# A sparse-attention decoder step: sampled queries broadcast by DMA, their logits eight units earlier

## The chip, the cores and the metric

The kernel is written for one Trainium2 chip and runs on one of its cores. Its time is the time of the whole program on the device in microseconds; the median of several runs counts. A core has TensorE (PE, matmuls and transposes into PSUM), VectorE (DVE), ScalarE (ACT), GpSimd (POOL) and SyncE (SP); the last two issue most of the DMAs here. Each engine works through its own list in order and waits on semaphores.

## The reference

One layer of a hybrid decoder, for 1024 prompt tokens and 8 sampled tokens (one each of 8 sequences with 2048 cached positions). Only the attention matters here. For each query an indexer has chosen 256 keys; the query attends over these alone:

```
q, k, v = project(x)                          # 8 heads of 64, rotary on a quarter of each head
idx = top_k(index_scores, 256)
ks, vs = rows idx of the keys and values      # samples: from the paged cache, or the sample's own new row
logits = einsum('bthd,btkhd->bthk', q, ks) * 64 ** -0.5
out = einsum('bthk,btkhd->bthd', softmax(logits), vs)
```

Everything is float32. Behind it come the merge of the branches, a layer norm, a router and a mixture of 32 experts.

## The kernel before

The program is a row of blocks with a barrier of all engines between two of them. `project_and_score` computes q, k, v and the index scores, `choose_keys_and_gate` picks the keys and computes the gates, `attend` is the attention, and `merge_route_and_experts` begins with loads of the gates (L1553) and matmuls with the weights `w_a` (L1643).

**Prompt.** `attend` goes over 32 units `(t, hp)`: tiles of 128 queries t = 7, 6, ... 0, and in each the four pairs of heads. Unit n of t has logits of 128 queries by (t+1)*128 keys for two heads. So units 0 to 3 have t = 7, units 8 to 11 t = 5, units 12 to 15 t = 4, units 16 to 19 t = 3, units 28 to 31 t = 0. All engines go over the same steps s = 0 to 33, as a pipeline written out by hand. In step s:

- TensorE: `make_logits(s)` (L1173), which waits until VectorE has read the logits of unit s-1; transposes of the probabilities of unit s-1 (`turn_probs`, L1187; for t of 4 and more, the keys from 512 on come at the end of the step); `weigh(s-2)` with the values (L1200), which waits at each new t until the output bank has been read; at the last pair of a t, `spread_shares` (L1213).
- VectorE: masks, scales and takes the bound of the logits of unit s (L1385, one operation for each of two heads, and a short read of the accumulator); at times a reciprocal (L1390); copies a share of unit s-1's transposed probabilities out of PSUM (L1296); `share_out` (L1372) at the last pair of a t.
- ScalarE: the other copies (L1296), the exponentials (L1312), a copy of the shares (L1323).

Logits lie in PSUM banks 0 and 2, and, from 512 keys (t of 4 and more) on, in banks 1 and 3 too.

**Samples.** Their work is set between the steps. GpSimd gathers the 256 chosen rows of K and of V of each sample b from the cache by indirect DMA, in two halves of 128 rows (L1132), and one own row from the new keys and values (L1137); it issues a few of them in each unit, when `wait_for_turn` says that the unit's probabilities have been copied: K in units 0 to 7, own K and the first halves of V in units 8 to 15, the second halves and own V in units 16 to 23. K of the first four samples lies where `w_a` is loaded later. With `narrow` = 16 the steps are: in steps 18 to 25, one sample each, TensorE spreads the query over 128 partitions by a matmul of a broadcast column with the identity, into bank 1 or 3 (`spread_query`, L1222), and VectorE multiplies it with K and sums over each head (`sample_logits`, L1345 and L1347, twice each). In step 26 the logits are transposed (L1230) and their maximum is taken, in 27 ScalarE exponentiates, in 28 VectorE scales, in 29 the probabilities are transposed (L1236), in 30 TensorE weighs V with them (L1247). Behind the loop ScalarE copies the result (L1326), TensorE transposes it (L1258), and VectorE picks it into `attnT` in sixteen small copies (L1411). TensorE ends with the first matmuls with `w_a` (L1285), which wait for the last `share_out`. SP loads `w_a` once the first four samples' logits are done.

Of the kernel before, what the change touches and what calls it, by code (L numbers as in the profile page):

```python
# [16 lines left out]
ALU = mybir.AluOpType  # L17
# [50 lines left out]

def project_and_score(nc, ins, outs, keep):

# [4 lines left out]
    with nc.cleanup_on_exit(), ExitStack() as ctx:  # L75
# [91 lines left out]
        def _(sp):  # L167
# [16 lines left out]
            for t in range(2, NT):  # L184
# [7 lines left out]
                         zs[2 * FEW:2 * FEW + N_SAMPLE, IDX_HEADS * HD:(IDX_HEADS + 1) * HD]).then_inc(few_out, 16)  # L192
            sp.dma_start(outs["v_all"][SEQ:, :], zs[3 * FEW:3 * FEW + N_SAMPLE, :]).then_inc(few_out, 16)
            for t in range(NT):
                j = t % 2
                if t == NT - 1:
                    sp.wait_ge(acc_full, 1 + 4 * NT)
                    for k in range(KC // 2, KC):
                        sp.dma_start(keep["w_uv"](k), ins["w_uv"][:, k, :]).then_inc(keep["w_uv_in"][k], 16)
                sp.wait_ge(roped, t + 2)  # L200
                sp.dma_start(outs["k_all"][t * P:(t + 1) * P, :], z[j][:, AW:2 * AW]).then_inc(stored[j], 16)
                sp.dma_start(outs["kidx_all"][t * P:(t + 1) * P, :], z[j][:, (ROPE_HEADS - 1) * HD:ROPE_HEADS * HD]).then_inc(stored[j], 16)
                sp.wait_ge(acc_read, AFTER_FEW + 5 * t + 5)
# [11 lines left out]
            sp.wait_ge(few_out, 48)  # L215
            sp.wait_ge(rest_in, 16)
# [171 lines left out]
        def _(act):  # L388
# [11 lines left out]
            def read(t, g):  # L400
                bank = FIRST_BANKS[g] if t == 0 else g % 2
                act.wait_ge(acc_full, 1 + 4 * t + g + 1)
                if g == 0 and t == 1:
                    act.wait_ge(few_out, 48)
                    act.wait_ge(turned_full, 1)
# [628 lines left out]
def attend(nc, ins, outs, keep, scratch):  # L1034


    SCALE = HD ** -0.5
    PAIRS = HEADS // 2
    n_qh = N_SAMPLE * HEADS
    with nc.cleanup_on_exit(), ExitStack() as ctx:  # L1040
# [3 lines left out]
        def sem(name):  # L1044
            return nc.alloc_semaphore(name)
# [14 lines left out]
        own_b = sb("own_b", [1, N_SAMPLE], I32)  # L1060
        own_row = sb("own_row", [2, N_SAMPLE], U32)
        lg = sb("lg", [P, 2, n_qh])
        prob_s = sb("prob_s", [n_qh, TOPK])
# [18 lines left out]
        dve_step = sem("a_dve_step")  # L1082
        q_spread = sem("q_spread")
        lg_ready = sem("lg_ready")
# [8 lines left out]
        narrow = order.index(3) * PAIRS  # L1093
        query_at = {narrow + 2 + b: b for b in range(N_SAMPLE)}
        MAX_AT, EXP_AT, PROBS_AT, TURN_AT, WEIGH_AT = (max(query_at) + n for n in (1, 2, 3, 4, 5))

# [23 lines left out]
        @block.sync  # L1120
        def _(sp):
            wait_for_gates_stored(sp)
            sp.dma_start(first[:], ins["first_masks"]).then_inc(const_in, 16)
            sp.dma_start(own_b[:], ins["rank"][:, 0:N_SAMPLE]).then_inc(own_in, 16)
            sp.wait_ge(lg_ready, N_SAMPLE // 2)
            sp.dma_start(keep["w_a"][:], ins["w_a"]).then_inc(w_a_in, 16)
            sp.wait_ge(w_a_in, 16)

        @block.gpsimd
        def _(pool):  # L1130
# [13 lines left out]

            for b in range(N_SAMPLE):
                wait_for_turn(b)
                for half in range(2):
                    gather(k_of, "cache_k", b, half, k_in)
            pool.wait_ge(own_ready, 1)
            pool.wait_ge(k_in, 32 * N_SAMPLE)  # L1150
            for b in range(N_SAMPLE):
                wait_for_turn(N_SAMPLE + b)
                gather_own(k_of, "k_all", b, k_in)
                gather(v_of, "cache_v", b, 0, v_in)
            pool.wait_ge(v_in, 16 * N_SAMPLE)
            for b in range(N_SAMPLE):
                wait_for_turn(2 * N_SAMPLE + b)
                gather(v_of, "cache_v", b, 1, v_in)
                gather_own(v_of, "v_all", b, v_in)
            pool.wait_ge(k_in, 48 * N_SAMPLE)  # L1160
# [3 lines left out]
        def _(pe):  # L1164
# [52 lines left out]

            def spread_query(b):
                if b >= 2:
                    pe.wait_ge(lg_ready, b - 1)  # L1220
                for k in range(AW // P):
                    mm = nc.tensor.matmul(ps[:, 1 + 2 * (b % 2), k * P:(k + 1) * P],  # L1222
                                          qT[:, k, SEQ + b:SEQ + b + 1].to_broadcast([P, P]), ident[:],
                                          start=True, stop=True)
                mm.then_inc(q_spread, 1)

            def turn_sample_logits():
# [24 lines left out]
            def turn_sample_out():  # L1252
                wait_copied(pe, len(chunks) - 2)
                wait_copied(pe, len(chunks) - 1)
                for g in range(2):
                    pe.wait_ge(s_copied, g + 1)
                    for k in range(AW // P):
                        mm = nc.tensor.transpose(ps[:, TURN + g, k * P:(k + 1) * P], product[g][:, k * P:(k + 1) * P], ident[:])  # L1258
                    mm.then_inc(s_turned, 1)

            for s in range(LAST):
                if s < N:
                    make_logits(s)
                if s in query_at:
                    spread_query(query_at[s])
                if s == MAX_AT:
# [3 lines left out]
                if s == WEIGH_AT:  # L1270
                    weigh_sample()
                if 0 <= s - 1 < N:
                    turn_probs(s - 1, 0)
# [4 lines left out]
                if 0 <= s - 1 < N and units[s - 1][0] >= 4:  # L1278
                    turn_probs(s - 1, 4)
            turn_sample_out()  # L1280
            pe.wait_ge(w_a_in, 16)
# [18 lines left out]
        def _(act):  # L1300
            for s in range(LAST):
# [22 lines left out]
            for g in range(2):  # L1324
                act.wait_ge(s_out, g + 1)
                nc.scalar.copy(product[g][:], ps[:, 1 + 2 * g, :]).then_inc(s_copied, 1)  # L1326

        @block.vector
        def _(dve):
# [39 lines left out]
            def share_out(t):  # L1369
# [4 lines left out]
                                        shares[:].rearrange("p (k q) -> p k q", q=P), ALU.mult).then_inc(out_read, 1)  # L1374

            for s in range(LAST):
                if s < N:
# [27 lines left out]
            for g in range(2):  # L1405
                dve.wait_ge(s_turned, g + 1)
                for k in range(AW // P):
                    for odd in range(2):
                        q0 = odd * HD
                        mine = ps[q0:q0 + HD, TURN + g, k * P:(k + 1) * P].rearrange("p (j h) -> p j h", h=32)  # L1410
                        nc.vector.tensor_copy(attnT[q0:q0 + HD, k, SEQ + 4 * g:SEQ + 4 * (g + 1)], mine[:, :, 2 * k + odd])  # L1411

# [1058 lines left out]
def build(nc, ins, outs, scratch):  # L2471
    with ExitStack() as whole:
# [4 lines left out]
        with ExitStack() as mixer:  # L2477
# [9 lines left out]
            with nc.sbuf_tensor("x_all", [P, KC, SEQ + N_SAMPLE], F32, side="right") as keep["x_all"], \  # L2487
# [10 lines left out]
                keep["made_out"] = [whole.enter_context(nc.semaphore(f"made_out{j}")) for j in range(2)]  # L2498
                project_and_score(nc, ins, outs, keep)
                choose_keys_and_gate(nc, ins, outs, keep, scratch)  # L2500
# [121 lines left out]
```

## Time and profile before

| what | value |
| --- | --- |
| runs of the program | 1389.69, 1389.03, 1385.95 us, median 1389.03 |
| the profiled execution | 1389.41 us |
| its span, first to last instruction | 1388.0 us |
| mean granted TensorE clock | 0.986 of full |
| attention stage | from 678 to 829.5 us |
| TensorE, VectorE busy over the span | 1321.8, 720.9 us |

The page of the profile gives busy times, the chain of work that ended last, and the costliest groups of instructions. L1173 is a line of the kernel. The timeline gives, for one instruction or a merged row of equal ones, the start, the duration, the engine, the line, what is written from what, and in brackets how long the engine stood idle before it and what released it.

### The profile page before, as it was taken

How to read it: one execution, taken by the hardware profiler on the slowest of the kernel's cores; microseconds unless marked ns; L12 is line 12 of the kernel's file. 1: busy time of each engine (PE TensorE's matmuls, PEld its weight loads, DVE VectorE, ACT ScalarE, POOL GpSimd, SP SyncE). 2: the span in 40 equal slices, each digit the busy share in tenths (PEclk: the TensorE clock that was granted, in tenths of full speed). 3: DMA queues.
4: the chain of work that ended last, by engine and by line, in shares of the span. 5: the costliest groups of instructions: out<-in, count | busy, mean ns of one | idle time of the engine just before them, and what ended most of it. 6: DMA issues, size and time to landing. Idle time of an engine off the chain costs nothing. (4 is left out here: it accounts for less than half of the span.)

```text
span 1388.0 us, 19213 instructions
## 1 busy us (share of the span) xinstructions
PE 1321.8 (95%) x6689; PEld 680.6 (49%) x6689; DVE 720.9 (52%) x1709; ACT 280.3 (20%) x621; POOL 245.0 (18%) x292
## 2 busy tenths in 40 slices
PE   8999999899999999999899989999978999999984
PEld 2444444445466666666577656544443333333321
DVE  0211123589898888998265863588881111111135
ACT  0100112322221111111356430000001111111124
POOL 2222000043420000021134400011112111111113
PEclk9999999999999999999999999999989999999997
DMA  9311002210031111110132319931137999999936
GB/s 326 98 52 62 17 17 77 94 50 1 0 109 69 69 68 69 68 68 32 34 100 62 125 34 318 388 127 31 38 114 256 365 408 406 406 412 411 394 143 255
DMA packets 70316, 214.13 MB, mean 154 GB/s; under 512 B 16059, under 2 KB 41915, under 8 KB 59866
## 3 DMA queue, kind: packets, MB, share of 16 engines
q1 hardware_dynamic: 56266, 184.74, 35.5%
q0 software_dynamic: 12688, 27.76, 5.8%
q8 instruction: 52, 0.85, 0.2%
q10 hardware_dynamic: 1280, 0.53, 0.2%
q14 instruction: 30, 0.25, 0.1%
HBM read 186.47 MB, written 34.65 MB: 159 GB/s over the span
## 5 line engine op out<-in xcount | busy, mean ns | idle before, releaser
L262 PE MATMUL ps_mixer<-front,x_all 128*128 128x512 f32 (+1 forms) x448 | 180.4, 557 | 1.7 <-ACT wi L413 1.7
L959 DVE TENSOR_SCALAR_CACHE_REDUCE front<-score,bound 128x384 bf16<-128x384 f32 (+2 forms) x198 | 173.9, 940 | 0.4 <-DVE bound L981 0.3
L262 PEld LDWEIGHTS ps_mixer<-front,x_all 128*128 128x128 f32 x448 | 83.2, 190 | 91.7 <-issue 78.7
L2102 PE MATMUL ps<-w_gate_up,w_o 128*32 128x512 f32 (+1 forms) x640 | 114.9, 597 | 1.7 <-DVE w_o L2186 1.7
L1672 PE MATMUL ps<-w_o,mergedT 128*128 128x512 f32 x256 | 116.5, 601 | 0.0
L2102 PE MATMUL ps<-w_a,w_o 128*64 128x512 f32 (+1 forms) x256 | 114.8, 602 | 0.0
L787 PE MATMUL ps_mixer<-x_all,front 128*128 128x344 f32 x384 | 114.4, 453 | 0.0
L787 PE MATMUL ps_mixer<-x_all,w_gate 128*128 128x344 f32 x384 | 113.3, 453 | 0.0
L2211 DVE TENSOR_TENSOR w_o<-w_o,ps 128x256 f32<-128x256 f32 x24 | 10.1, 421 | 165.7 <-ACT w_o L2166 165.7
L787 PEld LDWEIGHTS ps_mixer<-x_all,w_gate 128*128 128x128 f32 x384 | 72.7, 190 | 37.5
L787 PEld LDWEIGHTS ps_mixer<-x_all,front 128*128 128x128 f32 x384 | 72.6, 190 | 37.1
L959 DVE TENSOR_SCALAR_CACHE_REDUCE front<-score_s,bound 8x2049 bf16<-8x2049 f32 x33 | 77.0, 2334 | 0.0
L941 POOL TENSOR_TENSOR front<-front 128x344 f32<-128x344 f32 x24 | 28.6, 1193 | 241.6 <-ACT front L901 241.6
L1672 PEld LDWEIGHTS ps<-w_o,mergedT 128*128 128x128 f32 x256 | 46.0, 190 | 47.8 <-issue 47.8
L2102 PEld LDWEIGHTS ps<-w_gate_up,w_o 128*32 128x32 f32 (+1 forms) x640 | 33.5, 116 | 70.2 <-issue 70.2
L2080 POOL DMA_INDIRECT pair_out<-w_o,entries x24 | 25.1, 1044 | 233.4 <-DVE w_o L2218 233.4
L898 ACT ACTIVATE front<-ps_mixer,gate_bias 128x344 f32<-128x344 f32 x48 | 26.2, 547 | 177.0 <-PE ps_mixer L787 177.0
L1643 PE MATMUL ps<-attnT,w_a 128*128 128x344 f32 x186 | 56.0, 464 | 3.4 <-DVE mergedT L1792 1.9
L2134 PE MATMUL ps<-gates,w_o 128*32 128x512 f32 (+1 forms) x128 | 58.1, 597 | 0.5 <-ACT w_o L2171 0.5
L2134 PE MATMUL ps<-w_down,w_o 128*32 128x512 f32 (+1 forms) x320 | 58.3, 596 | 0.0
L735 PE MATMUL ps_mixer<-front,x_all 128*128 128x512 f32 x128 | 57.4, 592 | 0.0
L2102 PE MATMUL ps<-mergedT,w_o 128*32 128x512 f32 x384 | 56.5, 594 | 0.0
(349 smaller groups left out, 1894.7 us busy)
## 6 DMA issues: line engine op xcount, KB each, us to landing
w_gate_up<-in_w_gate_up SPq DMA_DIRECT2D x16, 2048.0 KB, 14.0
w_down<-in_w_down SPq DMA_DIRECT2D x16, 1024.0 KB, 15.5
w_a<-in_w_gate_up SPq DMA_DIRECT2D x8, 2048.0 KB
mergedT<-in_w_gate_up SPq DMA_DIRECT2D x8, 2048.0 KB
gates<-in_w_down SPq DMA_DIRECT2D x8, 1024.0 KB
mergedT<-in_w_down SPq DMA_DIRECT2D x8, 1024.0 KB, 9.4
front<-in_w_qkvi SPq DMA_DIRECT2D x7, 930.0 KB, 18.2
w_gate<-in_w_gate SPq DMA_DIRECT2D x4, 1280.0 KB, 6.2
```

The lines of the kernel that those rows point to most:

```text
L262: mm = nc.tensor.matmul(ps[:, g % 2, 0:c1 - c0], x_all[:, k, t * P:(t + 1) * P], w[:, k, c0:c1], start=(k == 0), stop=(k == KC - 1))
L735: mm = nc.tensor.matmul(ps[:, bank, :], x_all[:, k, t * P:(t + 1) * P], w_uv(k)[:, half * GW:(half + 1) * GW], start=(k == 0), stop=(k == ...
L787: mm = nc.tensor.matmul(ps[:, SETS[at % 2][which], 0:n], w_gate[j][:, which * KC + k, :], right[:, k, c0:c0 + n], start=(k == 0), stop=(k ...
L898: op = nc.scalar.activation(to, src, ACT.Sigmoid, bias=gate_bias[:, which, bass.ds(i * 2 + j, 1)])
L941: nc.gpsimd.tensor_tensor(m[:, 1, 0:n], m[:, 1, 0:n], m[:, 2, 0:n], ALU.mult).then_inc(multiplied, 1)
L959: V.tensor_scalar(waste[0:n, at - width:at], s, column(bound, g), None, compare, ALU.add, accum_out=column(number, g)).then_inc(taken, 1)
L1643: mm = nc.tensor.matmul(ps[:, FIRST_BANK + n % 3, 0:width], w_a[:, k, blk * P:(blk + 1) * P], attnT[:, k, c0:c0 + width], start=(k == 0), ...
L1672: mm = nc.tensor.matmul(ps[:, PROJECTED[i % 2][c], :], mergedT[:, k, t * P:(t + 1) * P], w_o[:, k, c * 512:(c + 1) * 512], start=(k == 0), ...
L2080: pool.indirect_dma_start(out=scratch["pair_out"].rearrange("t w q j d -> (t w q j) d"), out_offset=bass.IndirectOffsetOnAxis(ap=entries[: ...
L2102: mm = nc.tensor.matmul(ps[c0:c1, GU, :], rowsT[j][:, k, c0:c1], w_gu[b][:, k, :], start=(k == 0), stop=(k == KC - 1))
L2134: mm = nc.tensor.matmul(ps[c0:c1, 4 + 2 * j + c, :], hiddenT[j][:, k, c0:c1], w_dn[b][:, k, c * 512:(c + 1) * 512], start=(k == 0), stop=( ...
L2211: nc.vector.tensor_tensor(hidden[j], hidden[j], ps[:, GU, F:2 * F], ALU.mult).then_inc(hid, 1)
```

## The change

The sampled queries no longer pass through TensorE: `project_and_score` stores them in DRAM, and SP reads each back into all 128 partitions, into one of four new buffers. All of K, with the own rows, is gathered in units 0 to 8 and V in units 9 to 17. As the products no longer need banks 1 and 3, sampled logits are made in steps 10 to 17. The later sampled steps start at 19, and the copy, the transposes and the sixteen copies of the sampled output are steps 24 and 25 of the loop in place of its tail.

```
# project_and_score, SP, behind the stores of the samples' K, index and V rows
+            sp.dma_start(scratch["q_few"], zs[0:N_SAMPLE, :]).then_inc(few_out, 16)
# (the waits for few_out go from 48 to 64)

# attend
+    Q_AHEAD = 4
+        q_rows = [sb(f"q_rows{j}", [P, AW]) for j in range(Q_AHEAD)]
-        query_at = {narrow + 2 + b: b for b in range(N_SAMPLE)}
-        MAX_AT, EXP_AT, PROBS_AT, TURN_AT, WEIGH_AT = (max(query_at) + n for n in (1, 2, 3, 4, 5))
+        query_at = {narrow - N_SAMPLE + 2 + b: b for b in range(N_SAMPLE)}
+        MAX_AT, EXP_AT, PROBS_AT, TURN_AT, WEIGH_AT, COPY_AT, OUT_AT = (max(query_at) + 2 + n for n in range(7))
# SP, behind the load of own_b
+            for b in range(N_SAMPLE):
+                if b >= Q_AHEAD:
+                    sp.wait_ge(lg_ready, b - Q_AHEAD + 1)
+                sp.dma_start(q_rows[b % Q_AHEAD][:], scratch["q_few"][b:b + 1, :].to_broadcast([P, AW])
+                             ).then_inc(q_in[b % Q_AHEAD], 16)
# GpSimd, in place of three loops
+            def gather_all(first, to, cache, new, arrived):
+                for n in range(N_SAMPLE + 1):
+                    wait_for_turn(first + n)
+                    if n >= 1:
+                        pool.wait_ge(arrived, 48 * n - 16)
+                        gather_own(to, new, n - 1, arrived)
+                    if n < N_SAMPLE:
+                        for half in range(2):
+                            gather(to, cache, n, half, arrived)
             pool.wait_ge(own_ready, 1)
+            gather_all(0, k_of, "cache_k", "k_all", k_in)
+            gather_all(N_SAMPLE + 1, v_of, "cache_v", "v_all", v_in)
# TensorE: spread_query is gone; turn_sample_out, behind the loop before, is in it, into banks 1 and 3
+                if s == OUT_AT:
+                    turn_sample_out()
# ScalarE: the same two copies of the sampled result, behind the loop before
+                if s == COPY_AT:
+                    for g in range(2):
+                        act.wait_ge(s_out, g + 1)
+                        nc.scalar.copy(product[g][:], ps[:, 1 + 2 * g, :]).then_inc(s_copied, 1)
# VectorE, sample_logits
-                dve.wait_ge(q_spread, b + 1)
+                dve.wait_ge(q_in[b % Q_AHEAD], 16 * (b // Q_AHEAD + 1))
-                    step(nc.vector.tensor_tensor(product[half][:], k_of(b, half),
-                                                 ps[:, 1 + 2 * (b % 2), :], ALU.mult))
+                    step(nc.vector.tensor_tensor(product[half][:], k_of(b, half), q_rows[b % Q_AHEAD][:], ALU.mult))
# VectorE: the sixteen small copies, behind the loop before, as read_sample_out()
+                if s == OUT_AT:
+                    read_sample_out()
```

## Rows read from the trace of the kernel before

**Rows 1.** The page, busy time and share of the span.

```profile
PE 1321.8 (95%) x6689; PEld 680.6 (49%) x6689; DVE 720.9 (52%) x1709; ACT 280.3 (20%) x621; POOL 245.0 (18%) x292
```

**Rows 2.** Chain of waits from 600 to 900: start, us, what; its first piece.

```profile
829.49 0.33 SPq L1553
```

**Rows 3.** Timeline of the stage's end.

```profile
824.70 0.69 DVE L1372 TENSOR_TENSOR attnT<-ps,shares 128x512 f32<-128x512 f32 x1 [2.09 <-ACT shares L1323]
...
825.89 2.75 DVE L1411 COPY attnT<-ps 64x4 f32<-64x4 f32 x16 [0.50 <-PE ps L1258]
...
826.13 1.90 PE L1285 MATMUL ps<-attnT,w_a 128*128 128x344 f32 x6
```

**Rows 4.** Windows: length, busy us of PE, PEld, DVE, ACT, POOL; clock, DMA share, GB/s.

```profile
791.00:803.00 12.00, 10.56 (x106) 8.19 (x104) 11.69 (x29) 4.83 (x16) 5.67 (x6) 1.00 0.59 225
...
803.00:806.50 3.50, 1.04 (x10) 0.47 (x7) 3.40 (x8) 1.44 (x5) 0.00 (x0) 1.00 0.02 5
...
807.70:810.90 3.20, 3.20 (x22) 1.83 (x18) 1.83 (x8) 1.55 (x8) 0.00 (x0) 0.55 0.00 0
```

**Rows 5.** Timeline, VectorE in wide units: reads at t = 5, copies at t = 5 and 4.

```profile
735.56 0.96 DVE L1385 CUSTOM_DVE_ANT_0 probs<-ps,score 128x768 f32<-128x768 f32 x1 [0.28 <-PE ps L1173]
...
738.65 0.76 DVE L1296 COPY probsT<-ps 128x256 f32<-128x256 f32 x2 [1.25 <-PE ps L1187]
...
756.90 0.49 DVE L1296 COPY probsT<-ps 128x128 f32<-128x128 f32 x2 [1.49 <-PE ps L1187]
```

**Rows 6.** Timeline around step 18: a query's spread, reads, sampled products, next reads.

```profile
770.05 1.16 PE L1222 MATMUL ps<-ident,qT 128*128 128x128 f32 x8
...
772.26 0.08 DVE L1385 DVE_READ_ACCUMULATOR2_ANT low<- 128x1 f32 x1
...
772.87 0.68 DVE L1345 TENSOR_TENSOR product<-w_a,ps 128x512 f32<-128x512 f32 x1
...
775.63 0.68 DVE L1385 CUSTOM_DVE_ANT_0 probs<-ps,score 128x512 f32<-128x512 f32 x1
```

**Rows 7.** Timeline of TensorE: logits of unit 19, weighing of V, logits of unit 31.

```profile
773.03 1.13 PE L1173 MATMUL ps<-kT,qT 64*128 64x512 f32 x4
...
815.64 3.64 PE L1247 MATMUL ps<-v_sel,probT_s 128*32 128x512 f32 x32
...
819.95 0.49 PE L1173 MATMUL ps<-kT,qT 64*128 64x128 f32 x4
```

**Rows 8.** Waits from 678 to 830: us in total, times, the longest.

```profile
PE ps L1173 <- DVE low L1385: 5.4, 4, 3.3
...
PE ps L1230 <- DVE lg L1347: 2.4, 1, 2.4
...
PE ps L1200 <- DVE attnT L1372: 1.1, 1, 1.1
```

**Rows 9.** Timeline of GpSimd: the last K gather, and one that waited for earlier gathers.

```profile
730.70 0.95 POOL L1132 DMA_INDIRECT k_sel<-in_cache_k,rows  x1 [0.30 <-issue]
...
771.70 0.95 POOL L1132 DMA_INDIRECT v_sel<-in_cache_v,rows  x1 [2.65 <-DMA v_sel<-in_cache_v,rows]
```

**Rows 10.** DMA issues: times, KB each, us from issue to landing.

```profile
first_masks<-in_first_masks SPq DMA_DIRECT2D x1, 192.0 KB, 2.3
```

**Rows 11.** Two groups of VectorE: duration in ns min/median/max, first and last start.

```profile
L1795 DVE TENSOR_TENSOR mergedT<-mergedT,gates x24: 516/517/519, 832.9 to 888.5; 128x344 f32<-128x344 f32 x24
...
L1792 DVE TENSOR_TENSOR mergedT<-ps,gates x24: 509/517/518, 832.3 to 887.9; 128x344 f32<-128x344 f32 x24
```

**Rows 12.** Timeline: GpSimd and VectorE side by side, in two other stages.

```profile
611.90 4.42 DVE L995 TENSOR_TENSOR_SCAN front<-front 8x2049 f32<-8x2049 f32 x1
612.12 4.91 POOL L941 TENSOR_TENSOR front<-front 128x344 f32<-128x344 f32 x1 [15.28 <-ACT front L901]
...
913.72 1.13 POOL L1611 DMA_INDIRECT list_of<-entry,slot_out  x1 [0.20 <-issue]
913.98 0.42 DVE L1874 TENSOR_TENSOR attnT<-attnT 128x256 f32<-128x256 f32 x1
```

More of the change, by code:

```diff
@@ L66, with project_and_score @@
 V_BANK = 1
-def project_and_score(nc, ins, outs, keep):
+def project_and_score(nc, ins, outs, keep, scratch):
     BH = N_SAMPLE * IDX_HEADS
@@ L214, in _ @@
                 sp.wait_ge(stored[j], 48 * NT // 2)
-            sp.wait_ge(few_out, 48)
+            sp.wait_ge(few_out, 64)
             sp.wait_ge(rest_in, 16)
@@ L403, in read @@
                 if g == 0 and t == 1:
-                    act.wait_ge(few_out, 48)
+                    act.wait_ge(few_out, 64)
                     act.wait_ge(turned_full, 1)
@@ L1082, in attend @@
         dve_step = sem("a_dve_step")
-        q_spread = sem("q_spread")
+        q_in = [sem(f"q_rows_in{j}") for j in range(Q_AHEAD)]
         lg_ready = sem("lg_ready")
@@ L1143, in wait_for_turn @@
                 wait_copied(pool, chunk_of[n, 1, units[n][0] // 4 * 4])
[L1145 to L1148, printed above, removed]
-            pool.wait_ge(own_ready, 1)
[L1150 to L1159, printed above, removed]
+            def gather_all(first, to, cache, new, arrived):
[7 more added lines that the diff above has]
+                            gather(to, cache, n, half, arrived)
+            pool.wait_ge(own_ready, 1)
+            gather_all(0, k_of, "cache_k", "k_all", k_in)
+            gather_all(N_SAMPLE + 1, v_of, "cache_v", "v_all", v_in)
             pool.wait_ge(k_in, 48 * N_SAMPLE)
@@ L1216, in spread_shares @@
                 mm.then_inc(spread, 1)
[L1218 to L1225, printed above, removed]
             def turn_sample_logits():
@@ L1252, in turn_sample_out @@
             def turn_sample_out():
-                wait_copied(pe, len(chunks) - 2)
-                wait_copied(pe, len(chunks) - 1)
                 for g in range(2):
@@ L1257, in turn_sample_out @@
                     for k in range(AW // P):
-                        mm = nc.tensor.transpose(ps[:, TURN + g, k * P:(k + 1) * P], product[g][:, k * P:(k + 1) * P], ident[:])
+                        mm = nc.tensor.transpose(ps[:, 1 + 2 * g, k * P:(k + 1) * P], product[g][:, k * P:(k + 1) * P], ident[:])
                     mm.then_inc(s_turned, 1)
@@ L1263, in _ @@
                     make_logits(s)
-                if s in query_at:
-                    spread_query(query_at[s])
                 if s == MAX_AT:
@@ L1279, in _ @@
                     turn_probs(s - 1, 4)
-            turn_sample_out()
             pe.wait_ge(w_a_in, 16)
@@ L1323, in _ @@
                     nc.scalar.copy(shares[:], ps[:, SHARE, :]).then_inc(shares_in, 1)
-            for g in range(2):
-                act.wait_ge(s_out, g + 1)
-                nc.scalar.copy(product[g][:], ps[:, 1 + 2 * g, :]).then_inc(s_copied, 1)
         @block.vector
@@ L1374, in share_out, with read_sample_out @@
                                         shares[:].rearrange("p (k q) -> p k q", q=P), ALU.mult).then_inc(out_read, 1)
+            def read_sample_out():
+                for g in range(2):
+                    dve.wait_ge(s_turned, g + 1)
+                    for k in range(AW // P):
+                        for odd in range(2):
+                            q0 = odd * HD
+                            mine = ps[q0:q0 + HD, 1 + 2 * g, k * P:(k + 1) * P].rearrange("p (j h) -> p j h", h=32)
+                            nc.vector.tensor_copy(attnT[q0:q0 + HD, k, SEQ + 4 * g:SEQ + 4 * (g + 1)], mine[:, :, 2 * k + odd])
             for s in range(LAST):
@@ L1402, in _ @@
                     read_sample_probs()
+                if s == OUT_AT:
+                    read_sample_out()
                 if s >= 2 and units[s - 2][1] == PAIRS - 1:
                     share_out(units[s - 2][0])
[L1405 to L1411, printed above, removed]
 N_EXPERTS = 32
@@ L2498, in build @@
                 keep["made_out"] = [whole.enter_context(nc.semaphore(f"made_out{j}")) for j in range(2)]
-                project_and_score(nc, ins, outs, keep)
+                project_and_score(nc, ins, outs, keep, scratch)
                 choose_keys_and_gate(nc, ins, outs, keep, scratch)
@@ L2609 @@
     shapes = {"gate_a": [KC, P, SEQ + N_SAMPLE], "merged_b": [KC, P, SEQ + N_SAMPLE]}
-    shapes |= {"h": [TILES, P // 2, 2, D], "pair_out": [TILES, 2, P // 2, 2, D]}
+    shapes |= {"q_few": [N_SAMPLE, AW], "h": [TILES, P // 2, 2, D], "pair_out": [TILES, 2, P // 2, 2, D]}
     scratch = {k: nc.dram_tensor(k, v, F32, kind="Internal").ap() for k, v in shapes.items()}
```

## The prediction

> **What bounds the kernel now.** The page's first part says that the tensor engine is the busiest by far, 95% of the span [rows 1], so a saving elsewhere counts only where that engine waits or has less to do. The change touches the attention stage, which starts at 678 us. It is closed off behind: the chain of waits, read backwards from the merge stage, begins at 829.49 with the first load of gates, which the block boundary releases [rows 2]. Whatever the end of attention gains is therefore handed on whole. The last work before that boundary is a vector one, the sixteen little copies of the sampled output, 825.89 to 828.64, with TensorE finished at 828.03 [rows 3].
>
> Then the windows, for how full TensorE is by stretch, and which granted clock it has [rows 4]: 88% full in 791 to 803, in the middle of the sampled queries, 30% in 803 to 806.5, and after that a stretch at 0.55 of full clock, nearly all of it at the level of 1.2 GHz. Last, the timeline of a wide unit (t = 5 or 4) and a narrow one (t = 3 to 0). In a wide unit VectorE waits for TensorE, 0.28 us ahead of its reads and 1.25 to 1.49 ahead of its copies; in the narrow units with a sampled query VectorE has no such gaps, and the view of waits has TensorE waiting for it [rows 5 to 8]. So the sampled products, which are VectorE work, are now at a place where VectorE is the slower of the two, and TensorE has 1.0 us of spreading a query in each of these units on top.
>
> **Units 10 to 17 get the products.** VectorE's price per step, each from start to start. A pair of logit reads: an operation overlaps the next by 0.08, so the 0.96 row gives 2 x 0.88 + 0.08 = 1.84 at t = 5 and the 0.68 one 1.29 at t = 3; halfway between, 1.58 at t = 4 [rows 5, 6]. Copies of transposed probabilities: 0.76 at t = 5, 0.49 at t = 4, 0.61 for the one at t = 3 (772.26 to 772.87). The block of four sampled operations: 772.87 to 775.63 = 2.76 [rows 6]. share_out: 0.60, its 0.69 less the overlap [rows 3]; the reciprocal 0.12.
> The steps' sums, from the end of the reads of unit 11 to that of unit 18 (each is copies of the unit before, products, then the reads of the next unit): 0.76 + 2.76 + 1.58 = 5.10; with the reciprocal and copies at 0.76, 5.22; with share_out and copies at 0.49, 5.43; 4.83; 0.49 + 2.76 + 1.29 = 4.54; with the reciprocal, 4.66; 0.61 + 2.76 + 0.60 + 1.29 = 5.26. Together 35.04. VectorE's gaps in a wide step now, some 1.5 to 2.2 us [rows 5], are smaller than the block of 2.76, so it becomes the one that sets the pace. The copies of unit 9 can't start before 738.65 [rows 5], so the reads of unit 11 end at 738.65 + 0.74 + 2.76 + 1.84 = 743.99 and those of unit 18 at 779.03, where they now end at 772.34 [rows 6]: a loss of 6.7 us.
>
> **Is K there in time?** Now the last K gather is issued at 730.70; with the own rows gathered between, it comes about 1.5 us later (0.95 + 0.30, and a slower start), ends at 733.2 and lands 2.4 us after that: the row at 771.70 waited for exactly this, 2.65 us from the end of a gather to the next issue [rows 9]. Only then may the own row of sample 7 be gathered: 0.3 + 0.93, and another landing of 2.4, which is 739.3 to 740.2, where the first product wants K at 739.4. Bounds: 0, and 2.4 for one more landing. I take 0.8, because the sum of the rows ends just behind the need. Everything behind it on VectorE (reads of unit 11, and TensorE's logits of unit 12) is late by this too: 7.5 us lost.
>
> **Edits that I cost at nothing.** The query's store is one more issue on SP some microseconds before SP's next wait ends, and ScalarE's wait for it lies 18 us later. The broadcasts of 256 KB land in some 2.3 us (192 KB of first masks) [rows 10]; four are loaded ahead, and each later one has three steps, 15 us. SP waits in them for lg_ready, but nothing is queued behind except w_a, which comes earlier than now. V's gathers run on GpSimd at three operations (3.6 us) per unit of 4.5 to 5.4, and V is needed at unit 23 only. If that cover were gone, the 3.57 us of weighing V would start late by what is missing. The product changes its second operand from PSUM to SBUF: 344 columns take 0.517 us with a PSUM operand and 0.517 without [rows 11], so 0.68 stays. The Trainium skill ("VectorE: DVE Perf Modes", The TRN2 errata) has a fixed part of 58 cycles for SBUF sources and 120 for PSUM, by which sixteen products would be an estimated 1.0 us cheaper in all; the trace, with its two equal rows, doesn't agree, and the measurement decides.
>
> **Units 19 to 30 without the queries.** From the start of unit 19's logits to unit 31's is 819.95 - 773.03 = 46.92 us now [rows 7]. Gone are: seven spreads at 1.0 (1.16 with the pipeline's tail) = 7.0 [rows 6]; the waits for VectorE, 2.15 for the low bounds (5.4 less 3.29 at the stage's start, which stays), 2.4 for the last logits, and 1.1 for the output bank, 5.6 [rows 8]; the slow clock, 3.2 us at 0.55, or 1.4 [rows 4]. Transposing logits and probabilities and weighing V (3.64 [rows 7]) are merely moved from units 26 to 30 to units 19 to 23, in both cases on TensorE. New in unit 25: eight transposes, 1.0; the wait for ScalarE's two product copies (2 x 0.5 behind its exponentials), 0.5; and VectorE's sixteen small copies, 2.75, which hold back share_out of t = 2 and so TensorE's first weighing at t = 1: 1.1. I add 0.5 for the exponentials, which short units without other work wait for. 46.92 - 14.0 + 3.1 = 36.0. Unit 19 starts at 779.03 + 0.8 + 0.06 = 779.9, unit 31 at 815.9: 4.0 us earlier than now, all of the wide units' loss regained.
>
> **The tail.** Behind the last share_out (ends 825.39) stand only the w_a matmuls, 1.90: the end is 825.45 + 1.90 = 827.35 in place of 828.64, 1.3 us [rows 3]. The copies on ScalarE and the transposes fall away from there too, and no one waits for them.
>
> **Sum.** -4.0 - 1.3 = -5.3 us with a clock that is never lowered. But TensorE now has two new gaps: some 1.7 us at unit 12 (0.9 plus the wait for K) and 2.1 at unit 18, where VectorE needs 5.26 us and TensorE some 3.1, its 4.1 of now less the spread. A gap of 2.4 came before the fall of now [rows 4, 8]. Whether a shorter one does it no row shows; bounds 0 and 2 x 1.4 us. I take 0.8, between none and one fall. Forecast: -4.5. The profiled execution took 1389.41 (span 1388.0, 1.4 around it), which gives 1384.9; the median of the runs shown, 1389.03, lies 0.4 below it, which gives **1384.5**.
>
> **Rivals.**
> *It only breaks even* (1387, from 1385 to 1390). The narrow units are latency chains (logits, read, exponential, transpose), not TensorE-bound, and give back little more than the wide ones lose. For it: unit 31 and others have TensorE idle on exponentials. Against: 7.0 us of spreads are real TensorE work and vanish. If half the 5.6 us of waits come back and the clock falls twice, -5.3 + 2.8 + 2.8 = +0.3; if only one, -1.
> *It gains more* (1381). K arrives in time (-0.8), no fall, and the half microsecond for exponentials and the 1.1 at unit 25 are hidden: -5.3 - 2.4 = -7.7.
> *The products and GpSimd lock each other out; slower.* Each product now reads two SBUF operands, in just the stretch in which GpSimd issues the V gathers. A GpSimd operation whose fellows take 0.91 took 4.91 beside a 4.42 us scan of VectorE with two SBUF operands [rows 12]. Were VectorE the one held, by up to 0.95 in each of sixteen products, it would be 15 us, on the engine that sets the pace: 1400. It decides from 0.33 us per product. Against: an addition of two SBUF operands at 913.98 ran inside an indirect DMA's issue on GpSimd and took its usual 0.42, while the latter took 1.13 [rows 12]; so GpSimd pays, and it has room. The Trainium skill ("SBUF — State Buffer", SBUF: two separate sides) says that a VectorE operation with two SBUF inputs and a GpSimd operation that reads SBUF exclude each other, the first to start holding the port; by that rule this rival would hold; the scan's row agrees with it, the addition's doesn't.
> *The change doesn't do what it says*: if K lands a whole unit late, all that moves is moved by 4.8 us and the gain is nil; counted with break-even.
>
> **Chances.** Forecast (1382.5 to 1386) 0.52; break-even 0.27; more gain 0.10; lock-out, or three and more falls of the clock in the wide units, 0.11. Within 0.3% (4.2 us), about what a measurement of this kernel can tell from no change, the forecast falls on the faster side in some 0.38 of its 0.52, since it lies so near the bound. Faster 0.38 + 0.10 = 0.48; slower 0.10; same 0.42. The range reaches from the better case, with 0.7 us more for runs (the three differ by 3.7), to the worse end of break-even: 1380.5 to 1389.5.
>
> **What would show it.** Right: logits of unit 19 start near 780; units 11 to 17 have TensorE waiting for the low bounds and VectorE almost never idle; no PE row of the query spread; unit 31 starts near 816; no vector copies behind the last share_out; merge stage begins near 825. Wrong: products longer than 0.69, or VectorE waiting more than 1 us for K at unit 10; a granted clock under 1 within 740 to 800; TensorE idle on exponentials in units 20 to 30; V late at unit 23.

## The result, and the profile after

The changed kernel takes 1404.48 us (median of 4 runs, 1399.63 to 1407.62), beside 1388.78 for the kernel before on the same chip: a ratio of 1.011, 95% interval 1.0093 to 1.0126. It is slower by 1.1%, where 0.3% faster was forecast, and outside the range of 1380.5 to 1389.5. The profiled execution took 1406.12 us, 16.7 more than that of before.

The page's first part differs little from [rows 1]: TensorE has 6.7 us less to do and a slightly smaller share of a longer span.

```profile
PE 1315.1 (94%) x6625; PEld 671.8 (48%) x6625; DVE 720.3 (51%) x1709; ACT 280.6 (20%) x621; POOL 246.1 (18%) x292
```

The attention stage tells more. It starts at 676.21 with the first logits (678.04 before), and the merge stage behind it begins 16 us later than in [rows 2]:

```profile
845.54 0.33 SPq L1552
```

First the view of waits over 678 to 850 (us in total, times, the longest), to be read against [rows 8]:

```profile
POOL v_sel L1145 <- DMA v_sel<-in_cache_v,rows: 30.0, 7, 6.4
...
PE ps L1180 <- DVE low L1389: 15.8, 5, 10.9
POOL k_sel L1145 <- DMA k_sel<-in_cache_k,rows: 15.9, 4, 5.2
...
POOL w_a L1145 <- DMA w_a<-in_cache_k,rows: 10.7, 3, 3.6
DVE product L1341 <- DMA k_sel<-out_k_all,own_row: 10.1, 1, 10.1
PE ps L1245 <- DMA v_sel<-out_v_all,own_row: 8.6, 1, 8.6
```

Two single waits, 10.1 us of VectorE for the last own row of K and 8.6 us of TensorE for the last own row of V, are 18.7 us together. Neither exists before. The other rows give a reason: GpSimd itself waits, ahead of its gathers of own rows (L1145), fourteen times and 56.6 us (the view puts the other two of its sixteen such waits, 3.5 and 4.7 us, down to other releasers). GpSimd's timeline, which answers to [rows 9], shows the pattern of two samples near the start, and the last of K and of V:

```profile
702.49 0.93 POOL L1145 DMA_INDIRECT w_a<-out_k_all,own_row  x1 [3.52 <-DMA w_a<-in_cache_k,rows]
703.72 0.96 POOL L1140 DMA_INDIRECT w_a<-in_cache_k,rows  x1 [0.31 <-issue]
704.99 0.95 POOL L1140 DMA_INDIRECT w_a<-in_cache_k,rows  x1 [0.30 <-issue]
709.57 0.93 POOL L1145 DMA_INDIRECT w_a<-out_k_all,own_row  x1 [3.62 <-DMA w_a<-in_cache_k,rows]
...
746.32 0.93 POOL L1145 DMA_INDIRECT k_sel<-out_k_all,own_row  x1 [3.57 <-DMA k_sel<-in_cache_k,rows]
...
809.60 0.93 POOL L1145 DMA_INDIRECT v_sel<-out_v_all,own_row  x1 [3.67 <-DMA v_sel<-in_cache_v,rows]
```

In `gather_all` the wait for `48 * n - 16` stands between a sample's two big gathers, just issued, and its own row, and the next sample's gathers are queued behind it. So each sample costs two issues, an idle landing of 3.5 to 3.6 us in most cases, and the own row: 709.57 - 702.49 = 7.08 us. TensorE's units take 5.9 us at t = 7, 5.2 to 6.8 at t = 6 and 4.6 to 5.9 at t = 5. GpSimd falls behind in every unit, mostly by 1 to 2 us, once by 1.6 more (the own row at 725.24 waited 5.2 us), and issues the last own row of K at 746.32, where VectorE wants it landed at 748.34 - 10.11 = 738.23.

What the two waits then cost, in the timelines of VectorE and TensorE:

```profile
748.34 0.69 DVE L1341 TENSOR_TENSOR product<-w_a,q_rows 128x512 f32<-128x512 f32 x1 [10.11 <-DMA k_sel<-out_k_all,own_row]
749.06 0.69 DVE L1342 TENSOR_REDUCE lg<-product 128x8 f32<-128x512 f32 x1
```
```profile
753.00 2.51 PE L1180 MATMUL ps<-kT,qT 64*128 64x512 f32 x8 [10.86 <-DVE low L1389]
...
811.72 6.61 PE L1245 MATMUL ps<-v_sel,probT_s 128*32 128x512 f32 x32 [8.57 <-DMA v_sel<-out_v_all,own_row]
...
842.69 1.97 PE L1280 MATMUL ps<-attnT,w_a 128*128 128x344 f32 x6 [1.56 <-DVE attnT L1367]
```

The product itself is as short as in [rows 6]. Weighing V takes 6.61 us where [rows 7] have 3.64, and the windows (columns as in [rows 4]) say why: TensorE stands idle through each wait, the granted clock falls to 0.50 in it, the level of 1.2 GHz, and it is still there for part of the work that follows (0.67 and 0.58 are means over both levels).

```profile
748.30:753.00 4.70, 0.00 (x1) 0.00 (x1) 4.56 (x9) 0.90 (x2) 1.24 (x2) 0.50 0.47 143
753.00:758.00 5.00, 5.00 (x36) 3.58 (x38) 4.88 (x11) 2.46 (x7) 2.84 (x3) 0.67 0.12 36
...
811.50:819.00 7.50, 7.28 (x38) 2.21 (x38) 0.00 (x0) 0.10 (x1) 0.00 (x0) 0.58 0.01 2
```

The tail came out as forecast in form: no vector copies lie behind the last `share_out`, and the `w_a` matmuls close the stage (1.97, [rows 3] have 1.90).

### The profile page after: what moved, and what is told of

Same layout as the page of the kernel before. It is cut to its first block and busy times, and to the rows that moved or that the text cites. A ratio compares the mean times of both kernels' runs of the same rounds, so it can differ in the third digit from the quotient of the medians.

```text
span 1404.6 us, 19108 instructions
## 1 busy us (share of the span) xinstructions
PE 1315.1 (94%) x6625; PEld 671.8 (48%) x6625; DVE 720.3 (51%) x1709; ACT 280.6 (20%) x621; POOL 246.1 (18%) x292
## 5 line engine op out<-in xcount | busy, mean ns | idle before, releaser
L2210 DVE TENSOR_TENSOR w_o<-w_o,ps 128x256 f32<-128x256 f32 x24 | 10.1, 421 | 164.0 <-ACT w_o L2165 164.0
L1180 PE MATMUL ps<-kT,qT 64*128 64x512 f32 (+3 forms) x192 | 42.4, 548 | 18.3 <-DVE low L1389 15.8
```

The lines of the kernel that those rows point to most:

```text
L1180: mm = nc.tensor.matmul(ps[:, 2 * e + c // 512, 0:c1 - c], qT[e * HD:(e + 1) * HD, hp, t * P:(t + 1) * P], kT[e * HD:(e + 1) * HD, hp, c:c ...
```

## The experiments

Theory A: GpSimd's waits inside `gather_all` are the whole loss, and the rest of the change works as worked out. Its rivals are that the moved products, the broadcasts or the output in the loop cost something of their own. In what follows a stage time runs from the first logits of unit 0 to the first load of the gates: 829.49 - 678.04 = 151.45 us before, 845.54 - 676.21 = 169.33 after the change. A unit's time runs from the start of its logits to that of the next unit's. One thing varies from execution to execution where no edit reaches: units 0 and 1 take 11.2 to 11.5 us in the traces of the kernel before, the changed one, the first two experiments and the last, and 12.1 to 12.5 in the others, with a mean granted clock of 0.50 to 0.72 over 678 to 686 in place of 0.79 to 0.89. So about 1 us of a difference between two stages can come from there, and I name it where it does.

**The own rows one sample behind.** Each sample has its own semaphore, and its own row is issued behind the big gathers of the next sample, when its own have mostly landed. Nothing else of the change is touched.

```
 for n in range(N_SAMPLE + 1):
     wait_for_turn(first + n)
+    if n < N_SAMPLE:
+        for half in range(2):
+            gather(to, cache, n, half, arrived[n])
     if n >= 1:
-        pool.wait_ge(arrived, 48 * n - 16)
+        pool.wait_ge(arrived[n - 1], 32)
         gather_own(...)
-    if n < N_SAMPLE:
-        for half in range(2):
-            gather(to, cache, n, half, arrived)
```

> The changed kernel, with one edit: each sample has its own semaphores for K and V, and in each unit the two big gathers of a sample are issued ahead of the wait for the sample before and of its own row, so that a landing (3.6 us from the end of the last issue) no longer stands between two samples. Theory A (GpSimd waits for every landing, which makes a sample 7.06 us long where a wide unit is 5, and so K and V late): the 10.1 us wait of VectorE at unit 10 shrinks to 0 to 2, the 8.6 us wait of TensorE at unit 23 is gone, the slow weighing of V (6.6 us in place of 3.6) too, and the time falls from 1404.5 to 1382 to 1386. Rival B (the products are held by GpSimd's operations, or the wide units cost far more than VectorE's own work): the waits go, but the time stays above 1392. Rival C (gathers themselves land more slowly with more in flight): K is late again, 1390 to 1400.

1381.75 us (10 runs), 0.9967 of the kernel before, interval 0.9952 to 0.9981. One edit in GpSimd's order turns 1.1% slower into 0.3% faster, so theory A holds and the rest of the change is worth having. The stage takes 822.53 - 676.59 = 145.94 us, 5.5 less than before. In its waits neither K nor V appears for VectorE or TensorE, and GpSimd waits for a landing ahead of an own row twice, 6.0 us in all (the third row below stands ahead of a big gather, where the program waits for its turn alone):

```profile
PE ps L1184 <- DVE low L1395: 6.1, 6, 3.3
...
POOL v_sel L1145 <- DMA v_sel<-in_cache_v,rows: 6.0, 2, 3.1
...
POOL k_sel L1140 <- DMA k_sel<-in_cache_k,rows: 1.6, 1, 1.6
```

Set against the changed kernel, its stage is 23.4 us shorter. That splits at the units' starts: 10.2 between units 11 and 12 (the wait for K), 1.0 from there to unit 19, 11.6 between units 23 and 24 (8.6 of wait for V and 3.0 more of weighing), and 0.8 before unit 11. Elsewhere two differences of 1.6 us cancel: unit 19 is shorter in the changed kernel and unit 22 longer.

**K waited for sample by sample.** The changed kernel with GpSimd's order as it was, but each product waits for its own sample alone.

```
-    if b == 0:
-        dve.wait_ge(k_in, 48 * N_SAMPLE)
+    dve.wait_ge(k_in[b], 48)
```

> The changed kernel with GpSimd's order as it is, but a semaphore for each sample, and VectorE waits for K of the one sample that it multiplies, no more for all eight. K of sample b is in at about 696 + 7 b us, ahead of its product. Theory A (one chain of landings on GpSimd, sixteen samples of 7.06 us, sets when V is there, about 813): the wait at unit 10 vanishes, but TensorE then waits that much longer for V at unit 23, 15 to 19 us in place of 8.6, and the time is 1399 to 1404, nearly that of the changed kernel. Rival (the two waits are separate losses, of which each can be mended by itself): 1392 to 1395.

1405.66 us, ratio 1.0137 (1.0118 to 1.0155): nothing is gained. The wait for K is gone, and the one for V has grown by more than that; GpSimd's last own row is issued at the same time as in the changed kernel, 809.68 and 809.60.

```profile
PE ps L1247 <- DMA v_sel<-out_v_all,own_row: 20.1, 1, 20.1
```
```profile
809.68 0.93 POOL L1145 DMA_INDIRECT v_sel<-out_v_all,own_row  x1 [3.59 <-DMA v_sel<-in_cache_v,rows]
```

So the two waits can't be mended one by one on the side of the engine that waits. Both are set by one chain on GpSimd, and the first merely hid part of the second. By the medians the kernel lies 1.2 us above the changed one, where I had it at or below, but the two intervals overlap and its stage is 1.6 us shorter (167.76), so which of the two is slower is not shown. Its wait is now a single one of 20.1 us, with a granted clock of 0.66 over 790 to 820.

**The new order for V alone.** The edit of the first experiment for V; K's gathers stay as in the changed kernel.

```
-gather_all(0, k_of, "cache_k", "k_all", k_in)                 # order of the first experiment
+gather_all(0, k_of, "cache_k", "k_all", k_in, free=False)     # order of the changed kernel
```

> The changed kernel, where V's gathers are issued ahead of the wait for the sample before, as in the kernel that has both so, and K's gathers are as in the changed kernel. Theory A: VectorE still waits 10 us for K at unit 10, TensorE no longer for V; 1391 to 1394, that is 11 to 12 us less than the changed kernel (8.6 of wait and 3 of slow clock in the weighing of V). Rival (the clock falls at unit 10 and costs most): above 1397.

1396.04 us, ratio 1.0073 (1.0047 to 1.0098), some 2 above what I expected. V's wait is gone, K's is 9.8 us, and the stage is 159.25 us, 13.3 more than with both mended. Unit 11, with the wait in it, is 9.9 of that. Unit 12, behind it and at a lowered clock, takes 760.80 - 753.62 = 7.18 us, and 4.92 in the first experiment. The remaining 1.2 lie in units 0 and 1, which no edit touches.

```profile
DVE product L1347 <- DMA k_sel<-out_k_all,own_row: 9.8, 1, 9.8
```

**The gathers alone.** The kernel before (queries by TensorE, products in units 18 to 25, output in the tail) with the changed `gather_all`.

```
 # kernel before, GpSimd's three loops of gathers replaced by
+gather_all(0, k_of, "cache_k", "k_all", k_in)
+gather_all(N_SAMPLE + 1, v_of, "cache_v", "v_all", v_in)
```

> The kernel before, with the changed order of gathers alone (all K with own rows, then all V, each sample waiting for its landing); queries by TensorE at units 18 to 25 as before. Theory A: K is complete near 749 and is needed near 773, V near 813 and is needed at unit 30, near 816, so nothing waits: 1387 to 1391, the same as before. Rival (the gathers slow the other engines by themselves, by a port or by DMA traffic): above 1392, with longer VectorE operations in units 0 to 17.

1386.29 us (ten runs, one of them of 5560.28 us, which the ratio leaves out), ratio 0.9996 (0.998 to 1.0012). In its view of waits no row of VectorE or TensorE waits for K or V. The slow order of gathers costs nothing where K is wanted at unit 18 and V at unit 30. It needed the earlier products to make it late.

**The queries by DMA alone.** The kernel before with the query's store and broadcasts, without TensorE's spreads; products, gathers and tail stay.

```
-    if s in query_at:
-        spread_query(query_at[s])
...
-    product[half], k_of(b, half), ps[:, 1 + 2 * (b % 2), :]
+    product[half], k_of(b, half), q_rows[b % Q_AHEAD]
```

> The kernel before with one part of the change alone: the query rows come by DMA, TensorE's eight spreads are gone, and the sampled products stay at units 18 to 25, the gathers and the end as before. Theory A (VectorE sets the pace of those units: from 772.87 to 807.47 of the kernel before it has one gap, 0.64 us, so TensorE's 8 x 1.0 us is not what they wait for): 1384 to 1387 against the 1386.8 of the kernel before beside it, 0 to 3 us faster, with TensorE waiting for the low bounds by some 7 us in units 18 to 25 where it waits 5.4 now. Theory B (the spreads are TensorE work that the end sees in full): 7 us faster, 1379 to 1381. A third way: the new gaps of TensorE bring a lowered clock, 1387 to 1390. Products stay at 0.68 to 0.69 us by all three.

1388.11 us, ratio 1.001 (0.9995 to 1.0025): no change, and theory B is out. The stage is 151.52 us, against 151.45. From the start of unit 19 to that of unit 26 it is 29.82 us, against 30.21 with seven spreads in between: TensorE does less and waits more (the first row below). Unit 18, with the eighth spread, gives back 0.9 (3.11 for 4.04). From unit 26 on the stage then takes 1.3 us more, behind the wait of the second row and at a lower clock: the window of 800 to 810 has 0.66 here and 0.86 before, and four transposes take 1.06 us (third row) where they take 0.60. The missing spreads are not the cause as far as the runs show: the gathers alone, with all eight spreads, have 0.68 there, and units 26 and 27 are as long, 5.56 and 3.26 us.

```profile
799.43 0.70 PE L1181 MATMUL ps<-kT,qT 64*128 64x256 f32 x4 [1.01 <-DVE low L1381]
802.53 0.63 PE L1229 MATMUL ps<-ident,lg 128*64 128x128 f32 x2 [2.40 <-DVE lg L1343]
802.95 1.06 PE L1195 MATMUL ps<-ident,probs 128*128 128x128 f32 x4
```

**The output behind the loop again.** The kernel of the first experiment, its output turned in the tail.

```
 for s in range(LAST):
-    if s == OUT_AT:
-        turn_sample_out()
 ...
+turn_sample_out()        # and the copies of ScalarE and VectorE likewise
```

> The kernel with the big gathers issued ahead of the own rows (1381.75 us), with its sampled output copied and turned behind the last unit again, as in the kernel before. It prices the last part of the change. By the prediction's terms the turning inside the loop costs 1.0 + 0.5 + 1.1 us in unit 25 and spares 1.3 at the end, so without it the kernel is 1.3 us faster: 1380.5. The rival: in the loop the transposes and the small copies fill gaps of short units that wait for exponentials, so that only the end counts and the kernel gets 1.3 to 2 slower: 1383 to 1384.

1383.37 us (12 runs), ratio 0.9967 (0.9952 to 0.9982), the same ratio as with the output in the loop. The terms can be read apart, though. Units 25 and 26 take 2.90 and 2.23 us, against 4.21 and 3.03: the loop pays 2.1 us for turning the output, where the prediction had 2.6. (From the stage's start to unit 31 it is 134.9 us, against 137.4. But in these 2.5 us stand also 1.6 of unit 19, which the first experiment has at a lowered clock, and, the other way, 1.3 of units 0 and 1.) From unit 31 to the end it is 10.8, against 8.55: the tail pays 2.2, of which the prediction had 1.3; a granted clock of 0.83 in 810 to 820 is part of it, and the kernel before, with the same tail, needs 9.54. The move is a wash.

**Products in halves.** The kernel of the first experiment, one half of a sampled product in each of steps 3 to 18, waiting for its own sample.

```
-query_at = {narrow - N_SAMPLE + 2 + b: b for b in range(N_SAMPLE)}
+query_at = {3 + n: divmod(n, 2) for n in range(2 * N_SAMPLE)}     # sample, half
```

> The same kernel (1381.75 us), with each sampled product cut in two: one half (a product and its sum, 1.38 us of VectorE in place of 2.76) per step from step 3 to step 18, waiting for its own sample's K alone; the maximum and all that follows come one step later. Theory A (the wide units lose 6.7 us because the block of 2.76 is longer than VectorE's gap of 1.5 to 2.2, and 1.38 is shorter): units 10 to 17 run at the pace of the kernel before again, 4.7 to 5.0 us each, and nearly all of the loss comes back: 1374 to 1378. Rival B: the block lies on the way between a unit's copies and the next reads whatever its length, so the same VectorE time is lost, spread over more units: 1380 to 1383. A lesser one: the first half at step 3 waits for the own row of sample 0, which is issued near 696 and lands some 3 us later: 1 to 3 us of A's gain gone, 1376 to 1380, with a wait for K of that length in the waits.

1378.64 us, ratio 0.9937 (0.9912 to 0.9962). A second measurement of the same kernel:

> The kernel with halved sampled products once more, beside the next one on one chip, for a narrower interval of its gain: theory A 8 to 9 us below the kernel before (0.9935 to 0.9945 of its time); by rival B, had the first measurement been lucky, 5 us below, as with whole products (0.9965).

1376.56 us, ratio 0.9916 (0.9899 to 0.9933). The stage takes 141.9 and 141.8 us. From the start of unit 10 to that of unit 19 it is 38.3 us, with whole products 44.2, before 39.1, and units 3 to 9, which now have products too, are only 0.2 longer. So the time is not merely spread over more units, rival B is out, and no wait for K appears either. The stage as a whole gains some 4 us over whole products: units 19 to 22 are 1.7 shorter too, without the lowered clock of the first experiment's unit 19, but units 0 and 1 are 1.1 longer in this execution, and units 23 to 30 are 2.1 longer, which is the next experiment's matter. The timeline of VectorE shows a half's two operations in what had been its gap, and 0.31 us of gap left:

```profile
738.50 0.76 DVE L1296 COPY probsT<-ps 128x256 f32<-128x256 f32 x2 [0.31 <-PE ps L1198]
739.18 0.68 DVE L1345 TENSOR_TENSOR product<-w_a,q_rows 128x512 f32<-128x512 f32 x1
739.89 0.69 DVE L1346 TENSOR_REDUCE lg<-product 128x8 f32<-128x512 f32 x1
740.50 0.95 DVE L1394 CUSTOM_DVE_ANT_0 probs<-ps,score 128x768 f32<-128x768 f32 x1
```

**The output in two steps.** The halved kernel, eight of the small copies in each of two steps.

```
-if s == OUT_AT:
-    read_sample_out()            # g = 0 and 1
+if s - OUT_AT in (0, 1):
+    read_sample_out(s - OUT_AT)  # one g; TensorE's transposes likewise
```

> The kernel with halved sampled products, and the sampled output also turned and copied in two halves, eight small copies of VectorE (1.37 us) in each of two steps in place of sixteen (2.74 us) in one. In the trace of the halved kernel these sixteen, 798.38 to 801.12, are followed by TensorE's only long wait of the short units, 1.83 us for the low bounds at 801.96, and by slower rows (weighing eight blocks 1.12 in place of 0.66 us) until 807. Theory A (a VectorE block in a step costs what it is longer than the step's gap, and the fall of the clock behind the wait costs 1 to 2 more): 1.5 to 3 us faster than the halved kernel beside it. Rival B (the short units wait for exponentials anyway, or another gap brings the fall): within 0.7 us of it.

1377.15 us, ratio 0.9917 (0.99 to 0.9933), the same as the halved kernel beside it. The profiled execution agrees with A inside the stage. That takes 138.6 us against 141.8; 0.8 of the 3.2 lie in units 0 and 1, and 2.3 in units 26 to 29, 9.6 us for 11.9 (both traces of the halved kernel have 11.9). TensorE's wait at unit 28 is not there, and the 1.83 us of the kernel beside it (first fence) has become a row with no idle time (second):

```profile
802.15 0.49 PE L1184 MATMUL ps<-kT,qT 64*128 64x128 f32 x4 [1.83 <-DVE low L1394]
```
```profile
800.13 0.49 PE L1184 MATMUL ps<-kT,qT 64*128 64x128 f32 x4
```

But its whole time is only 2.1 us below the other's profiled one, and its median is 0.6 above, with an interval of 2.3 us to either side. Whether the gain of 2.3 us holds from run to run is left open. The best kernel is thus the halved one, with the output in one step or in two, 0.6 to 0.8% below the kernel before and some 2% below the changed one.

## Why the prediction was wrong

The step that failed is **Is K there in time?**, and with it V's cover in **Edits that I cost at nothing**. There I took the gathers as issues: two and an own row, 3.6 us per unit of 4.5 to 5.4, with one landing of 2.4 us at the end of K. The loop has that landing once per sample. It is also longer: 3.5 to 3.6 us from the end of a gather to the next issue, where the row that I took mine from [rows 9] has 2.65. There one gather was awaited and here a pair; that this is the reason fits and was not tested. Some 7.1 us per sample against units of mostly 5 to 6 is not hidden but accumulates over eight samples; V starts behind K and accumulates in turn. I looked only at the last sample, and put the wait at 0.8 us with an upper bound of 2.4; it was 10.1. I named V's price, that weighing would start late by what is missing, and gave it no chance; it was 8.6, and 3.0 more for the clock. The first experiment removes both, and the kernel comes out 5.0 us faster, where 4.5 was forecast. That this is so close is in part luck, as the terms below miss in both directions.

**Units 10 to 17 get the products.** With K in time: the block is 737.72 to 740.49, 2.77 us (2.76 forecast), and VectorE sets the pace. Unit 19 starts 100.2 us into the stage, 5.2 later than before. The forecast had 6.9, of which 0.8 was the wait for K. Halving the block brings all of it back. That bears out the mechanism: what a wide unit loses is the block's excess over VectorE's gap.

**Units 19 to 30 without the queries.** 813.98 - 776.77 = 37.2 us in the first experiment, 36.0 forecast, 46.9 before. The size is right, but one term can't be counted by itself. Seven spreads stood there as 7.0 us of real TensorE work that vanishes; removed by themselves they give 0.4 (29.82 for 30.21). VectorE set the pace of these units, so TensorE gets its microseconds back only when the products leave too.

**The tail.** 8.55 us from unit 31 to the end, 9.54 before: 1.0 gained, 1.3 forecast. Turning the output in the loop costs 2.1, so the part of the change taken by itself gives nothing (the experiment with the output behind the loop).

**Sum.** +5.2 - 9.7 - 1.0 = -5.5 us in the stage, -5.3 forecast with no fall of the clock; -4.5 with one. The medians have 5.0. One fall is there (0.85 in 770 to 780), behind a wait of 1.81 us in step 18, and unit 19 takes 4.93 us with it. The changed kernel has the same wait and no fall behind it, and its unit 19 takes 3.29. So a fall costs 1.6 us here, where I had 1.4, and whether it comes differs between executions: it is in the first three experiments, and not in the changed kernel nor in the one with the output behind the loop. First the two rows of the first experiment, then those of the changed kernel:

```profile
775.56 1.09 PE L1211 MATMUL ps<-probsT,early 128*64 128x128 f32 x16 [1.81 <-DVE attnT L1373]
776.77 1.86 PE L1184 MATMUL ps<-kT,qT 64*128 64x512 f32 x4
```
```profile
787.16 1.09 PE L1207 MATMUL ps<-probsT,early 128*64 128x128 f32 x16 [1.81 <-DVE attnT L1367]
788.38 1.13 PE L1180 MATMUL ps<-kT,qT 64*128 64x512 f32 x4
```

**Edits that I cost at nothing**, other than V's: store and broadcasts caused no wait; no row of VectorE or SP waits for them. A broadcast took a median of 3.7 us to land, where I had 2.3 from a smaller load, and had 15 us of cover.

```profile
q_rows<-q_few SPq DMA_DIRECT2D x8, 256.0 KB, 3.7
```

**The rivals.** *The change doesn't do what it says* had the right place, K late, and the wrong length: I stopped at one unit and folded it into break-even. It was two units, and then V. *Lock-out* is out: the products take what they took, and that its price of 1400 lies nearest to the measured time is chance. In the first experiment, where GpSimd issues V's gathers beside them, the groups of instructions show (busy us, mean ns of one):

```profile
L1140 POOL DMA_INDIRECT v_sel<-in_cache_v,rows x16 | 17.5, 1096 | 13.4 <-DVE probsT L1296 10.4 <-issue 2.7 <-DMA v_sel<-in_cache_v,rows 0.3
...
L1347 DVE TENSOR_TENSOR product<-k_sel,q_rows 128x512 f32<-128x512 f32 x8 | 5.5, 687 | 0.1
```

The products keep their 0.687 us; it is the gathers that get longer. Twelve of V's sixteen gathers are issued up to 765, among the products, and take 1.13 to 1.18 us; the last four, from 770 on, start with no product under way and take 0.94 to 0.96. The kernel with the queries by DMA alone shows what lengthens them. Its products stand at the same steps as before, and only their second operand has moved from PSUM to SBUF. Of V's gathers there the seven beside products take 1.15 to 1.17 us and the nine ahead of them 0.94 to 0.98, while the kernel before has 0.95 to 0.98 for all sixteen. First that experiment's row, then the one of before:

```profile
L1140 POOL DMA_INDIRECT v_sel<-in_cache_v,rows x16 | 16.7, 1043 | 14.8 <-DVE probsT L1293 9.4 <-issue 2.7 <-DMA v_sel<-in_cache_v,rows 2.7
```
```profile
L1132 POOL DMA_INDIRECT v_sel<-in_cache_v,rows x16 | 15.4, 961 | 18.1 <-DVE probsT L1296 13.0 <-DMA v_sel<-in_cache_v,rows 2.6 <-issue 2.4
```

The very first gather of the stage takes 1.13 in both of these, with no product near; why is open. The Trainium skill ("SBUF — State Buffer", SBUF: two separate sides) says that of a VectorE operation with two SBUF inputs and a GpSimd operation that reads SBUF the later one is blocked for the whole of the other. By that rule a product that starts just behind a gather would wait for it. In the first experiment the product at 772.05 starts 0.08 us into a gather of 0.95 and takes its usual 0.68, so this row does not agree.

## What to carry to other kernels

A wait in the middle of a queue costs its length once per round, and everything behind it comes that much later each time; so for each loop of DMAs work out the period of the loop, issues plus the landing it waits for, and compare it with the period of the work that consumes it, before looking at the last transfer. Where a gather depends on one just issued, put the next item's gathers between them. And when an engine's work is removed from a stretch, ask first whether that engine sets the pace there; a block moved into an engine's gap cost next to nothing here once it was shorter than the gap, so try cutting it until it is.

## What the hardware showed

- The landing of a pair of indirect gathers (two of 128 rows) held GpSimd for 3.3 to 3.8 us behind the end of the second issue nearly all through the stage of the changed kernel, and for 5.2, 5.8 and 6.4 us three times (the own rows at 725.24, 763.75 and 773.72; SP issued the 2 MB load of `w_a` at 767.63, which can explain the last alone; what lengthened the others is open). With that load issued at 756.09, in the second experiment, one such wait was 10.1 us. The Trainium skill ("DMA: Bandwidth & Descriptors", Anatomy of one DMA — SWDGE (gpsimd) path) gives some 2.0 us plus the bytes at 436 GB/s, an estimated 2.6 us for one such gather of 256 KB and 3.2 for the two taken as one; the rows here are above it.
- A wait of TensorE costs more than its length: behind 10.9 us of it the row of eight logit matmuls of unit 12 took 2.51 us, where the one of unit 13 took 1.35, and behind 8.6 us the weighing of V took 6.61 in place of 3.64, at mean granted clocks of 0.67 and 0.58.
- The same wait does not always bring the clock down. Behind 1.81 us in step 18 unit 19 took 4.9 us in three executions and 3.29 in the changed kernel; a trace of one execution can thus differ from the next by 1.6 us at one place.
- The issue of a gather on GpSimd takes 0.94 to 0.98 us, and 1.15 to 1.17 beside sampled products that read two SBUF operands; beside the same products with one operand in PSUM it stays at 0.96. The products take 0.68 to 0.69 us in both.
